# Norms and turns tile by tile, natural projections ahead of compress, dense tiles added during the last rows

## The chip, the cores and the metric

The kernel runs on one core of a Trainium2 chip. The time is device microseconds of one execution; the numbers compared are medians of several runs.

The engines are TensorE (PE, matmuls and transposes, here called turns; PEld is its weight load), VectorE (DVE), ScalarE (ACT), GpSimd (POOL) and SyncE (SP), which issues most DMAs. Each runs its own list of instructions in order and they meet by semaphores. Everything is fp32.

## The reference

A decoder layer for 512 tokens of width 1024: a combined projection, attention branches, and a retrieval of single-neuron experts (PEER), each after an RMSNorm, and a gated embedding at the end.

```python
h  = RMSNorm(x) ; z = h @ W_in
A  = sliding-window (128) GQA with per-head sinks and T5 relative bias
B  = compressed + selected blocks + sliding window (512), gated per head
x += W_o( sigmoid(gA) * (A @ W_upA) + sigmoid(gB) * (B @ W_upB) )
x += PEER(RMSNorm(x))
x += sigmoid(RMSNorm(x) @ W_pg) * (p @ W_ple)
out = RMSNorm(x)

def compress_blocks(t, pos, w1, w2):      # for B's compressed keys and values
    ...
    return jax.nn.gelu(flat @ w1) @ w2
```

## The kernel before

The 512 tokens are four tiles of 128 rows (TILES = 4), the width is KC = 8 chunks of 128. All orders are written out by hand: each engine has one function, and its instructions stand in program order.

**Start.** SP loads the x tiles, small constants, the bias table's two parts, then weight blocks of 512 KB. The blocks (wpack) go through a ring of RING = 5 places; block b is issued when block b - 5 has been used, which `used_up` expresses as a semaphore and a count. After block 0, SP waits for the bias rows, stores them and loads 16 bias tiles from them, before block 1. The PE makes the bias rows first (lines 1256 and 1257). ACT squares the four tiles (line 543) and takes one square root for all four (548). The DVE copies the bias rows out, fills `candno` (771), and scales the tiles (776). The PE turns them, chunk by chunk (1263), and ACT copies each chunk out to hT (552).

**Projections.** Thirteen blocks give z transposed (line 1272, ZT = 13, 8 matmuls each). For compress, the DVE builds windows of keys and values (788), and the PE multiplies them with eight blocks of w1 (1285), with 62 columns a matmul; four blocks are waited for at once and given back at once, one half (kv) after the other. ACT applies gelu (559). Then come the natural projections, values and head gates with tokens on the rows (1295): four blocks, all waited for first, 8 matmuls for each of the four tiles. The second compress matmuls (1301, 1304) follow, the DVE copies them out (793, 794), and the PE waits for that ahead of the first scores.

**Attention.** 32 batches: scores on the PE (1326), softmax on DVE, ACT and GpSimd, turned probabilities (1340) and values (1355). Between them the PE makes parts of the merge gates (1382). Then `up`, `project_out` (1415), which adds to x by `add_mixer` on the DVE (892), and `peer_norm`: ACT squares and roots, the DVE scales (899), the PE turns (1428), and queries (1453) follow.

**PEER.** Tiles 0 and 1 (NG = 2) gather rows of u and v, 512 KB for each of 128 picks a tile, by GpSimd's indirect DMAs (523) into SLOTS = 8 places; the DVE takes a product for each u row (1075) and adds each weighted v row (1110). A slot is gathered anew when its row has been used. Tiles 2 and 3 use all experts by dense matmuls: 128 chunks of scores (1542), then 128 chunks of values (1553), the matrix streamed by SP. At chunk 59 of the scores the PE turns the picks that the DVE numbered (1515). While rows of tile 1 are added (`accumulate(1, k)`, k = 0 to 127), dense tiles 2 and 3 are finished, and `add_dense` adds them to x.

**Tail.** In the order tile 0, 2, 3, 1 (`ORDER`; o counts them): ACT's square and root (`tail_norm`, 641, 643), the PE's turn (1480), the DVE's copy times gain (`tail_turned`, 1022), gate matmuls (1489), embedding matmuls (1503), ACT's sigmoid (650), the DVE's product and add (`tail_add`, 1030, 1033), ACT's last norm (656, 658), the last scaling (`tail_out`, 1039) and the store. `close(1)` ends tile 1's sum.

## Time and profile before

| | us |
|---|---|
| median of 3 runs | 1711.44 |
| the runs | 1711.39 to 1716.0 |
| the profiled execution | 1713.18 |
| its span in the trace | 1711.3 |
| PE busy | 1621.1 |
| DVE busy | 1064.0 |
| POOL busy | 619.8 |
| ACT busy | 431.0 |
| mean granted clock of the PE | 0.978 |

The span runs from the first to the last instruction; the execution's own time has a little around it. Busy times overlap between engines. The chain that ended last follows the work back from the last instruction, at each step to what released it. The granted clock is 1.00 at 2.4 GHz and 0.50 at 1.2 GHz. Up to 22 us the trace has no event of the clock, and the rows there say 1.00 whatever it was. A matmul in fp32 has two records.

### The profile page before, as it was taken

Reading aid. Unit: us, or ns where it says so; the run is one execution under the profiler, and the core shown is the slowest. Engines: PE = TensorE matmul, PEld = TensorE weight load, DVE = VectorE, ACT = ScalarE, POOL = GpSimd, SP = SyncE. Lnnn points to the kernel's source line nnn. Section 1 sums busy time; section 2 is a strip of 40 time slices with the busy share of each in tenths; the row PEclk is TensorE's granted clock in tenths of the full one; section 3 lists DMA queues with packets and bytes.
Section 4 is the critical chain, followed back from the end, with each engine's and each line's share of the span. In section 5 each row is a group of like instructions: output and inputs, shape, how many; then the busy total and the mean of one; then the engine's idle time right before and its main releaser. Section 6 shows DMA issues by size and latency. Waiting matters only on the chain.

```text
span 1711.3 us, 18283 instructions
## 1 busy us (share of the span) xinstructions
PE 1621.1 (95%) x6294; PEld 1052.1 (61%) x6294; DVE 1064.0 (62%) x2428; ACT 431.0 (25%) x1255; POOL 619.8 (36%) x650
## 2 busy tenths in 40 slices
PE   6988999998999799999989999999999999999957
PEld 3446454446588488888879999994444444444323
DVE  1010344442236999999968999997555556676772
ACT  3000444332011112111147777760000000000013
POOL 0000344460000144344445555555443344464620
PEclk9997999999999899999999999999999999999979
DMA  6231211004444699999989999999999999999940
GB/s 219 74 111 49 87 50 38 25 1 148 148 135 136 236 355 350 379 398 365 372 330 408 403 403 402 407 402 407 409 409 409 410 409 409 409 409 410 410 197 37
DMA packets 132552, 477.69 MB, mean 279 GB/s; under 512 B 14779, under 2 KB 15803, under 8 KB 132460
## 3 DMA queue, kind: packets, MB, share of 16 engines
q0 software_dynamic: 73728, 268.47, 40.0%
q1 hardware_dynamic: 58732, 208.06, 32.6%
q8 instruction: 50, 0.82, 0.2%
q14 instruction: 42, 0.34, 0.1%
HBM read 472.24 MB, written 4.24 MB: 278 GB/s over the span
## 4 chain that ended last, share of the span: by engine, by line
PE 65%; DMA 24%; DVE 4%; POOL 3%; issue 2%; ACT 1%; another core or an unknown queue 1%; SPq 0%; ACTq 0%; DVEq 0%
PE psum L1542 25%; DMA arena<-in_v,eidx 22%; PE psum L1453 6%; PE psum L1382 6%; PE psum L1272 5%; PE psum L1531 3%; PE psum L1415 3%; PE psum L1403 3%; PE psum L1489 2%; POOL arena L523 2%; PE psum L1340 2%; PE psum L1355 2%; PE psum L1295 1%; PE psum L1326 1%; PE psum L1285 1%
## 5 line engine op out<-in xcount | busy, mean ns | idle before, releaser
L1542 PE MATMUL psum<-arena 128*128 128x256 f32 x2048 | 455.2, 380 | 6.8 <-ACT arena L682 6.1
L1553 PE MATMUL psum<-arena 128*128 128x512 f32 x1024 | 440.8, 592 | 3.3 <-DMA arena<-in_vd 2.2
L523 POOL DMA_INDIRECT arena<-in_u,eidx x256 | 252.9, 988 | 474.7 <-DVE dots L1075 238.9
L1542 PEld LDWEIGHTS psum<-arena 128*128 128x128 f32 x2048 | 385.4, 191 | 57.4 <-issue 6.5
L523 POOL DMA_INDIRECT arena<-in_v,eidx x256 | 259.6, 1014 | 264.3 <-DVE arena L1110 147.8
L1553 PEld LDWEIGHTS psum<-arena 128*128 128x128 f32 x1024 | 194.2, 190 | 248.7 <-issue 242.5
L1110 DVE SCALAR_TENSOR_TENSOR arena<-arena,wts 128x1024 f32<-128x1024 f32 x182 | 233.2, 1285 | 118.9 <-DMA arena<-in_v,eidx 117.5
L1075 DVE CUSTOM_DVE_ANT_0 arena<-psum,arena 128x1024 f32<-128x1024 f32 x256 | 299.5, 1220 | 1.3 <-DVE arena L946 0.3
L501 POOL TENSOR_SCALAR arena<-arena 128x256 f32<-128x256 f32 (+4 forms) x128 | 105.9, 847 | 282.2 <-DVE arena L842 224.6
L1382 PE MATMUL psum<-arena 128*128 128x512 f32 x256 | 118.4, 605 | 0.0
L1453 PE MATMUL psum<-arena 128*128 128x256 f32 x512 | 113.0, 379 | 1.5 <-ACT arena L612 1.5
L1110 DVE SCALAR_TENSOR_TENSOR psum<-arena,wts,psum 128x1024 f32<-128x1024 f32 x57 | 73.5, 1289 | 52.7 <-DMA arena<-in_v,eidx 52.7
L1453 PEld LDWEIGHTS psum<-arena 128*128 128x128 f32 x512 | 96.2, 190 | 14.5 <-ACT arena L612 2.0
L705 ACT ACTIVATE arena<-arena 128x128 f32<-128x128 f32 x256 | 105.0, 488 | 0.0
L1272 PE MATMUL psum<-arena 128*128 128x512 f32 x208 | 89.5, 593 | 1.2 <-ACT arena L552 1.2
L682 ACT ACTIVATE arena<-psum 128x256 f32<-128x256 f32 (+31 forms) x126 | 41.1, 327 | 187.4 <-PE psum L1542 115.3
L641 ACT ACTIVATE arena<-arena 128x1024 f32<-128x1024 f32 x4 | 4.2, 1056 | 311.4 <-DVE arena L1117 252.3
L697 ACT ACTIVATE arena<-iota,arena 128x128 f32<-128x128 f32 x256 | 81.4, 395 | 0.0
L1382 PEld LDWEIGHTS psum<-arena 128*128 128x128 f32 x256 | 46.0, 189 | 55.5 <-issue 54.4
L588 ACT ACTIVATE arena<-arena 128x256 f32<-128x256 f32 (+4 forms) x128 | 59.8, 469 | 55.2 <-DVE arena L829 43.6
L1272 PEld LDWEIGHTS psum<-arena 128*128 128x128 f32 x208 | 39.4, 190 | 50.7 <-issue 49.3
L1531 PEld LDWEIGHTS psum<-arena 128*128 128x128 f32 x512 | 67.2, 192 | 3.3
(175 smaller groups left out, 1400.6 us busy)
## 6 DMA issues: line engine op xcount, KB each, us to landing
arena<-in_ut SPq DMA_DIRECT2D x128, 512.0 KB
arena<-in_vd SPq DMA_DIRECT2D x128, 512.0 KB
arena<-in_wpack SPq DMA_DIRECT2D x105, 512.0 KB
arena<-in_u,eidx POOLq DMA_INDIRECT x256
arena<-in_v,eidx POOLq DMA_INDIRECT x256
arena<-in_w_pg SPq DMA_DIRECT2D x8, 512.0 KB
arena<-in_x SPq DMA_DIRECT2D x4, 512.0 KB, 4.9
arena<-bias_rows SPq DMA_DIRECT2D x8, 256.0 KB, 5.6
```

Source lines behind the costliest of these rows:

```text
L501: last = G.tensor_scalar(sw[:, i % 3, r, 0:w], sw[:, i % 3, r, 0:w], scl[:, i, r:r + 1], None, ALU.mult)
L523: G.indirect_dma_start(out=row_slot(n), out_offset=None, in_=a["v"] if values else a["u"], in_offset=bass.IndirectOffsetOnAxis(ap=eidx[:, ...
L697: last = A.activation(hot2[:, g % 2, j, :], iota[:, :], ACT.Abs, scale=-1.0, bias=pickT[:, 1, tok:tok + 1])
L705: last = A.activation(hot2[:, g % 2, j, :], hot2[:, g % 2, j, :], ACT.Relu, scale=pickT[:, 3, tok:tok + 1], bias=pickT[:, 2, tok:tok + 1])
L1075: V.tensor_tensor_reduce(out=row_slot(n), in0=dot_rows[t], in1=row_slot(n), scale=1.0, scalar=0.0, op0=ALU.mult, op1=ALU.add, accum_out=do ...
L1110: V.scalar_tensor_tensor(to, row, w, to, ALU.mult, ALU.add).then_inc(row_used, 1)
L1272: last = T.matmul(ps[j % 8], blk(j)[:, k * P:(k + 1) * P], hT[:, k, :], start=(k == 0), stop=(k == KC - 1))
L1382: last = T.matmul(ps[4], blk(B_MG + m)[:, k * P:(k + 1) * P], hT[:, k, :], start=(k == 0), stop=(k == KC - 1))
L1453: last = T.matmul(ps[4 + p % 2][:, jj * HT:(jj + 1) * HT], blk(b)[:, k * P:(k + 1) * P], h2T[:, k, :], start=(k == 0), stop=(k == KC - 1))
L1531: last = T.matmul(mix_bank(g)[:, j * P:(j + 1) * P], hot1[:, g % 2, j, :], hot2[:, g % 2, j, :], start=True, stop=True)
L1542: last = T.matmul(chunk_scores(c), u[:, k * P:(k + 1) * P], h2T1[:, k, :], start=(k == 0), stop=(k == KC - 1))
L1553: last = T.matmul(ps[VALUE_BANK[t] + h], mixed[:, c, t * P:(t + 1) * P], stream[:, c % SRING, h * HALF:(h + 1) * HALF], start=(c == 0), st ...
```

## The change

The change moves work on four engines. (1) At the start ACT takes a root of a constant before x is there; ACT squares tiles 0 and 2, the DVE tiles 1 and 3; root, scaling and turning are made tile by tile. The bias matmuls move behind projection block 0, and SP's wait for the bias rows behind block 4. The bias table lies elsewhere, since its old place is written earlier now. (2) The natural projections come ahead of compress; they go by k in the outer loop, over four PSUM banks, and give back a block after each. Compress takes each block as it comes and gives it back when used, over two banks. The second compress matmuls stand behind the first two batches' scores and gate parts, and the DVE's copies of them behind batch 1's scores. (3) `peer_norm` has a root and a reciprocal for each tile, `turn` waits for one tile at a time, and for tiles 2 and 3 the scaling stands ahead of the second part of numbering the experts. (4) `add_dense` comes at rows 106 and 108 instead of 120 and 122, and the steps of the tail for tiles 2 and 3 follow among the rows. ACT's last norm of tile 2 moves ahead of the norm of tile 1.

```diff
-B_W1 = ZT
-B_NAT = B_W1 + 8
-B_MG = B_NAT + NATB
+B_NAT = ZT
+B_W1 = B_NAT + NATB
+B_MG = B_W1 + 8
...
             if b < ZT:
                 return proj_ready, b + 1
-            if b < B_NAT:
-                return cmp_hidden_ready, 2 * ((b - B_W1) // 4) + 2
+            if b < B_W1:
+                return (nat_block_used, b - B_NAT + 1) if b < B_W1 - 1 else (proj_ready, ZT + TILES)
             if b < B_MG:
-                return proj_ready, ZT + TILES
+                kv, part = divmod(b - B_W1, 4)
+                return (cmp_block_used, 3 * kv + part + 1) if part < 3 else (cmp_hidden_ready, kv + 1)
...
-                if b == 0:
+                if b == RING - 1:
...
-            for t in range(TILES):
+            def first_root(t):
+                A.activation(stat[:, 4 + t:5 + t], stat[:, t:t + 1], ACT.Sqrt, scale=1.0 / D,
+                             bias=epsc[:, :]).then_inc(rms_ready, 1)
+
+            A.activation(stat[:, 63:64], epsc[:, :], ACT.Sqrt)
+            for t in (0, 2):
                 act.wait_ge(x_loaded[t], 16)
                 norm_rows(t, 0, [early[:, i, :] for i in range(TILES)])
-            A.activation(stat[:, 4:8], stat[:, 0:4], ACT.Sqrt, scale=1.0 / D, bias=epsc[:, :]).then_inc(rms_ready, 1)
+                if t == 2:
+                    act.wait_ge(squares_ready, 1)
+                    first_root(1)
+                first_root(t)
+            act.wait_ge(squares_ready, 2)
+            first_root(3)
...
-            for j in range(4):
-                act.wait_ge(cmp_hidden_ready, j + 1)
-                A.activation(gT[:, j // 2, j % 2, :], ps[1 + j][:, 0:GROUPS * NCMP], ACT.Gelu_apprx_tanh).then_inc(cmp_gelu_ready, 1)
...
+            for kv in range(2):
+                act.wait_ge(cmp_hidden_ready, kv + 1)
+                for hb in range(2):
+                    last = A.activation(gT[:, kv, hb, :], hidden(kv, hb), ACT.Gelu_apprx_tanh)
+                last.then_inc(cmp_gelu_ready, 1)
...
-                A.activation(stat[:, 12 + t0:12 + t1], stat[:, 8 + t0:8 + t1], ACT.Sqrt, scale=1.0 / D,
-                             bias=epsc[:, :]).then_inc(rms_ready, 1)
+                    A.activation(stat[:, 12 + t:13 + t], stat[:, 8 + t:9 + t], ACT.Sqrt, scale=1.0 / D,
+                                 bias=epsc[:, :]).then_inc(rms_ready, 1)
...
             tail_gate(1)
+            tail_last_norm(1)
             tail_norm(3)
-            tail_last_norm(1)
             tail_gate(2)
...
+            def first_square(t):
+                dve.wait_ge(x_loaded[t], 16)
+                V.tensor_tensor_reduce(out=early[:, t, :], in0=xs[:, t, :], in1=xs[:, t, :], scale=1.0, scalar=0.0,
+                                       op0=ALU.mult, op1=ALU.add, accum_out=stat[:, t:t + 1]).then_inc(squares_ready, 1)
+
+            def first_norm(t):
+                dve.wait_ge(rms_ready, t + 1)
+                after(V.reciprocal(stat[:, 24 + t:25 + t], stat[:, 4 + t:5 + t]))
+                V.tensor_scalar(early[:, t, :], xs[:, t, :], stat[:, 24 + t:25 + t], None, ALU.mult).then_inc(rows_normed, 1)
+
+            first_square(1)
+            first_norm(0)
+            first_square(3)
+            for t in range(1, TILES):
+                first_norm(t)
...
+            def compressed_out():
+                dve.wait_ge(cmp_made, 1)
...
+                if i == 1:
+                    compressed_out()
...
-                dve.wait_ge(rms_ready, 2 + (t0 > 0))
-                after(V.reciprocal(stat[:, 28 + t0:28 + t1], stat[:, 12 + t0:12 + t1]))
                 for t in range(t0, t1):
+                    dve.wait_ge(rms_ready, TILES + t + 1)
+                    after(V.reciprocal(stat[:, 28 + t:29 + t], stat[:, 12 + t:13 + t]))
...
             add_mixer(3)
+            peer_norm(2, 4)
             number_low(0, 1)
-            number_high(0, 0)
-            peer_norm(2, 4)
-            for pair in range(1, 4):
+            for pair in range(4):
                 number_high(0, pair)
             publish(0, 4, 8, 0, 8)
...
-                if k == 120:
+                if k == 106:
                     add_dense(2)
-                if k == 122:
+                if k == 108:
                     add_dense(3)
                     tail_scale(1)
-                if k == 124:
+                if k == 110:
                     tail_turned(1)
-                if k == 126:
                     tail_scale(2)
+                if k == 112:
+                    tail_turned(2)
+                if k == 122:
+                    tail_add(1)
+                if k == 125:
+                    tail_out(1)
             close(1)
-            tail_turned(2)
-            tail_add(1)
             tail_scale(3)
-            tail_out(1)
             tail_turned(3)
             tail_add(2)
             tail_out(2)
...
-            pe.wait_ge(rel_loaded, 32)
             pe.wait_ge(pool_consts_set, 6)
-            pe.wait_ge(mask_row_set, 1)
-            T.matmul(ps[6][0:2 * HEADS, :], relb[:, :], hot[:, 0:HALF], start=True, stop=True)
-            T.matmul(ps[7][0:2 * HEADS, 0:P], relb[:, :], hot[:, HALF:S + P], start=True, stop=True).then_inc(bias_rows_ready, 1)
-            pe.wait_ge(bias_rows_out, 1)
-
-            pe.wait_ge(rows_normed, TILES)
-            for k in range(KC):
-                for t in range(TILES):
+            for t in range(TILES):
+                pe.wait_ge(rows_normed, t + 1)
+                for k in range(KC):
                     last = T.transpose(ps[k][:, t * P:(t + 1) * P], early[:, t, k * P:(k + 1) * P], ident[:, :])
-                last.then_inc(rows_turned, 1)
-
-            pe.wait_ge(hT_ready, KC)
+                    if t == TILES - 1:
+                        last.then_inc(rows_turned, 1)
+
             for j in range(ZT):
                 arrive(j)
+                if j == 6:
+                    pe.wait_ge(bias_rows_out, 1)
                 if j >= 8:
                     pe.wait_ge(proj_out, j - 7)
                 for k in range(KC):
+                    if j == 0:
+                        pe.wait_ge(hT_ready, k + 1)
                     last = T.matmul(ps[j % 8], blk(j)[:, k * P:(k + 1) * P], hT[:, k, :],
                                     start=(k == 0), stop=(k == KC - 1))
                 last.then_inc(proj_ready, 1)
+                if j == 0:
+                    pe.wait_ge(rel_loaded, 32)
+                    pe.wait_ge(mask_row_set, 1)
+                    T.matmul(ps[6][0:2 * HEADS, :], relb[:, :], hot[:, 0:HALF], start=True, stop=True)
+                    T.matmul(ps[7][0:2 * HEADS, 0:P], relb[:, :], hot[:, HALF:S + P], start=True,
+                             stop=True).then_inc(bias_rows_ready, 1)
+
+            pe.wait_ge(proj_out, ZT + TILES - 8)
+            for k in range(KC):
+                if k % 2 == 0:
+                    arrive(B_NAT + k // 2)
+                w = blk(B_NAT + k // 2)[:, (k % 2) * HALF:(k % 2) * HALF + NAT_COLS]
+                for t in range(TILES):
+                    last = T.matmul(ps[(ZT + t) % 8][:, 0:NAT_COLS], hT[:, k, t * P:(t + 1) * P], w,
+                                    start=(k == 0), stop=(k == KC - 1))
+                    if k == KC - 1:
+                        last.then_inc(proj_ready, 1)
+                if k % 2 and k < KC - 1:
+                    last.then_inc(nat_block_used, 1)
 
             for kv in range(2):
                 pe.wait_ge(windows_ready, 4 * kv + 4)
                 if kv == 0:
                     pe.wait_ge(proj_out, 11)
-                for b in range(4):
-                    arrive(B_W1 + 4 * kv + b)
+                else:
+                    pe.wait_ge(proj_out, 11 + TILES)
+                for l in range(LPAIR):
+                    b = B_W1 + 4 * kv + l // 4
+                    if l % 4 == 0:
+                        arrive(b)
+                    for hb in range(2):
+                        w = blk(b)[:, (l % 4) * CMP_HID + hb * P:(l % 4) * CMP_HID + (hb + 1) * P]
+                        last = T.matmul(hidden(kv, hb), w, cm[:, kv, l, :],
+                                        start=(l == 0), stop=(l == LPAIR - 1))
+                    if l == LPAIR - 1:
+                        last.then_inc(cmp_hidden_ready, 1)
+                    elif l % 4 == 3:
+                        last.then_inc(cmp_block_used, 1)
+
+            def compress():
+                pe.wait_ge(cmp_gelu_ready, 2)
                 for hb in range(2):
-                    for l in range(LPAIR):
...
-                    last.then_inc(cmp_hidden_ready, 1)
-
-            for b in range(NATB):
-                arrive(B_NAT + b)
-            for t in range(TILES):
-                j = ZT + t
-                for k in range(KC):
-                    w = blk(B_NAT + k // 2)[:, (k % 2) * HALF:(k % 2) * HALF + NAT_COLS]
-                    last = T.matmul(ps[j % 8][:, 0:NAT_COLS], hT[:, k, t * P:(t + 1) * P], w,
-                                    start=(k == 0), stop=(k == KC - 1))
-                last.then_inc(proj_ready, 1)
-
-            pe.wait_ge(cmp_gelu_ready, 4)
...
-            last.then_inc(cmp_made, 1)
...
+                last.then_inc(cmp_made, 1)
...
-            pe.wait_ge(cmp_out, 1)
-            pe.wait_ge(proj_out, 11 + TILES)
...
+            pe.wait_ge(cmp_gelu_ready, 1)
             for i in range(2):
                 queries_keys(i)
                 for part in range(4):
                     gate_part(i, part)
+            compress()
+            pe.wait_ge(cmp_out, 1)
             for i in range(len(BATCH)):
...
             def turn(h):
-                pe.wait_ge(rows_normed, TILES + 2 * h + 2)
-                for b in range(4):
-                    for kk in range(2):
-                        k = 2 * b + kk
-                        for t in range(2):
+                for t in range(2):
+                    pe.wait_ge(rows_normed, TILES + 2 * h + t + 1)
+                    for b in range(4):
+                        for kk in range(2):
+                            k = 2 * b + kk
                             last = T.transpose(ps[4 * h + b][:, (2 * kk + t) * P:(2 * kk + t + 1) * P],
                                                hn[2 * h + t][:, k * P:(k + 1) * P], ident[:, :])
-                    last.then_inc(rows_turned, 1)
+                        if t:
+                            last.then_inc(rows_turned, 1)
 
```

The PE from the start to the first turned probabilities, before (the L numbers are lines; the matmul with 16 rows is of the bias rows, 128x408 is natural, 128x62 compress, 64x62 and 31x64 its second part):

```order
L1256 MATMUL psum<-arena,relb 16x512
L1257 MATMUL psum<-arena,relb 16x128
L1263 MATMUL psum<-ident,arena 128x128 x32
L1272 MATMUL psum<-arena 128x512 x104
L1285 MATMUL psum<-arena 128x62 x64
L1295 MATMUL psum<-arena 128x408 x32
L1301 MATMUL psum<-arena,small 64x62 x2
L1304 MATMUL psum<-small,arena 31x64 x4
L1326 MATMUL psum<-arena 128x128 x4
L1382 MATMUL psum<-arena 128x512 x4
```

The same stretch now:

```order
L1293 MATMUL psum<-ident,arena 128x128 x32
L1306 MATMUL psum<-arena 128x512 x8
L1312 MATMUL psum<-arena,relb 16x512
L1313 MATMUL psum<-arena,relb 16x128
L1306 MATMUL psum<-arena 128x512 x96
L1322 MATMUL psum<-arena 128x408 x32
L1341 MATMUL psum<-arena 128x62 x64
L1376 MATMUL psum<-arena 128x128 x4
L1430 MATMUL psum<-arena 128x512 x4
L1376 MATMUL psum<-arena 128x128 x4
L1430 MATMUL psum<-arena 128x512 x4
L1351 MATMUL psum<-arena,small 64x62 x2
```

The bias matmuls went behind eight projection matmuls, the natural projections ahead of compress, and compress's second part behind two batches' scores and gates.

The DVE between the added output of tiles 2 and 3 (128x512 x4) and the end of numbering, before (the scaling of the norm is the SCALAR_TENSOR_TENSOR x2):

```order
L892 TENSOR_TENSOR arena<-arena,psum 128x512 x4
L975 TENSOR_TENSOR arena<-candno,arena 128x640
L977 TENSOR_TENSOR arena<-arena 128x640
L978 TENSOR_REDUCE arena<-arena 128x4x8
L975 TENSOR_TENSOR arena<-candno,arena 128x800
L977 TENSOR_TENSOR arena<-arena 128x800
L978 TENSOR_REDUCE arena<-arena 128x2x8
L897 RECIPROCAL stat<-stat 128x2
L899 SCALAR_TENSOR_TENSOR arena<-arena,stat 128x1024 x2
```

And now:

```order
L927 TENSOR_TENSOR arena<-arena,psum 128x512 x4
L933 RECIPROCAL stat<-stat 128x1
L934 SCALAR_TENSOR_TENSOR arena<-arena,stat 128x1024
L933 RECIPROCAL stat<-stat 128x1
L934 SCALAR_TENSOR_TENSOR arena<-arena,stat 128x1024
L1010 TENSOR_TENSOR arena<-candno,arena 128x640
```

Six instructions of the numbering moved from ahead of the two scalings to behind them.

The DVE's last rows, before (128x1024 with weights is a row; L1050 the dense add, L1022 the turned copy, L1117 the last sum, L1030 and L1033 gate product and add):

```order
L1110 SCALAR_TENSOR_TENSOR arena<-arena,wts 128x1024 x30
L1050 TENSOR_TENSOR arena<-arena,psum 128x512 x2
L1110 SCALAR_TENSOR_TENSOR arena<-arena,wts 128x1024 x2
L1050 TENSOR_TENSOR arena<-arena,psum 128x512 x2
L1017 RECIPROCAL stat<-stat 128x1
L1110 SCALAR_TENSOR_TENSOR arena<-arena,wts 128x1024 x2
L1022 TENSOR_TENSOR arena<-psum,small 128x512 x2
L1110 SCALAR_TENSOR_TENSOR arena<-arena,wts 128x1024 x2
L1017 RECIPROCAL stat<-stat 128x1
L1110 SCALAR_TENSOR_TENSOR arena<-arena,wts 128x1024
L1117 TENSOR_TENSOR arena<-arena 128x1024
L1022 TENSOR_TENSOR arena<-psum,small 128x512 x2
```

And now, from the second dense add on:

```order
L1085 TENSOR_TENSOR arena<-arena,psum 128x512 x2
L1052 RECIPROCAL stat<-stat 128x1
L1144 SCALAR_TENSOR_TENSOR arena<-arena,wts 128x1024 x2
L1057 TENSOR_TENSOR arena<-psum,small 128x512 x2
L1052 RECIPROCAL stat<-stat 128x1
L1144 SCALAR_TENSOR_TENSOR arena<-arena,wts 128x1024 x2
L1057 TENSOR_TENSOR arena<-psum,small 128x512 x2
L1144 SCALAR_TENSOR_TENSOR arena<-arena,wts 128x1024 x10
L1065 TENSOR_TENSOR arena<-arena,psum 128x512 x2
L1068 TENSOR_TENSOR arena<-arena 128x1024
L1144 SCALAR_TENSOR_TENSOR arena<-arena,wts 128x1024 x3
```

The dense adds stand 14 rows earlier, and a second turned copy, a gate product, an add and a last scaling have come in among the rows.

## Rows read from the trace of the kernel before

**Rows 1.** The page: shares of the chain; the costliest groups, the DVE's products.

```profile
PE 65%; DMA 24%; DVE 4%; POOL 3%; issue 2%; ACT 1%; another core or an unknown queue 1%; SPq 0%; ACTq 0%; DVEq 0%
...
L1075 DVE CUSTOM_DVE_ANT_0 arena<-psum,arena 128x1024 f32<-128x1024 f32 x256 | 299.5, 1220 | 1.3 <-DVE arena L946 0.3
```

**Rows 2.** The chain in order of time: start, duration, what.

```profile
15.09 2.75 DVE arena L776 x4
...
17.98 3.66 PE psum L1263 x16
...
24.79 89.53 PE psum L1272 x208
...
114.32 7.10 PE psum L1285 x64
...
127.68 13.90 PE psum L1285 x64
...
148.08 23.93 PE psum L1295 x64
...
548.78 27.48 PE psum L1415 x64
...
863.34 7.43 another core or an unknown queue
...
1652.36 27.47 PE psum L1489 x64
```

**Rows 3.** Timeline, 0 to 24 us: start, duration, engine, line, count [idle <-releaser].

```profile
4.51 1.28 ACT L543 ACT_TABLE_LOAD   x1 [4.51 <-DMA arena<-in_x]
...
10.51 1.28 ACT L548 ACT_TABLE_LOAD   x1
...
13.52 0.31 SPq L434 DMA_DIRECT2D bias_rows<-arena  x1
...
23.23 50.25 SPq L431 DMA_DIRECT2D arena<-in_wpack  x11
```

**Rows 4.** Line 423, x's DMAs: issue in ns, first and last start; landing.

```profile
L423 SPq DMA_DIRECT2D arena<-in_x x4: 392/422/432, 0.7 to 2.1; - x4
...
DMA to landing us min/median/max: 3.7/4.9/6.2
```

**Rows 5.** Stretches: window, busy of PE, PEld, DVE, ACT, POOL, clock, DMA, GB/s.

```profile
118.00:121.50 3.50, 3.41 (x31) 3.27 (x30) 0.00 (x0) 0.15 (x2) 0.00 (x0) 1.00 0.00 0
...
137.00:142.00 5.00, 4.56 (x22) 4.37 (x21) 0.00 (x0) 0.22 (x1) 0.00 (x0) 0.50 0.00 0
...
620.00:640.00 20.00, 20.00 (x103) 17.83 (x102) 19.59 (x27) 3.17 (x8) 7.73 (x9) 1.00 0.98 388
```

**Rows 6.** Timeline, the first scores on the PE.

```profile
173.76 0.72 PE L1326 MATMUL psum<-arena 64*128 64x128 f32 x8 [0.82 <-DVE arena L794]
```

**Rows 7.** Timeline, norms of tiles 2 and 3, and the picks' turn.

```profile
578.25 0.29 ACT L606 ACTIVATE stat<-stat,epsc 128x2 f32<-128x2 f32 x1
...
585.42 3.46 PE L1428 MATMUL psum<-ident,arena 128*128 128x128 f32 x16 [9.17 <-DVE arena L899]
...
589.56 10.63 PE L1453 MATMUL psum<-arena 128*128 128x256 f32 x48 [0.69 <-ACT arena L612]
...
857.53 0.41 PE L1515 MATMUL psum<-ident,arena 128*128 128x128 f32 x2 [0.48 <-issue]
```

**Rows 8.** Timeline, last 100 us: dense end, last rows, sum, add, last scaling.

```profile
1615.08 8.85 PE L1553 MATMUL psum<-arena 128*128 128x512 f32 x20 [1.52 <-DMA arena<-in_vd]
...
1617.80 23.04 DVE L1110 SCALAR_TENSOR_TENSOR arena<-arena,wts 128x1024 f32<-128x1024 f32 x18 [0.72 <-DMA arena<-in_v,eidx]
...
1640.75 1.28 DVE L1050 TENSOR_TENSOR arena<-arena,psum 128x512 f32<-128x512 f32 x2
...
1685.49 1.22 DVE L1033 TENSOR_TENSOR arena<-arena 128x1024 f32<-128x1024 f32 x1
...
1707.03 1.28 DVE L1039 SCALAR_TENSOR_TENSOR arena<-arena,stat 128x1024 f32<-128x1024 f32 x1
```

37 lines of the change are left out of this document (17 added, 20 removed).

## The prediction

> **What bounds the kernel now.** I read the chain of work that ended last first, because the shares of busy time are averages over stages that have different limits. It spends 65% of the span on TensorE (PE) and 24% on DMA [rows 1]. So a microsecond is worth something where that chain is on the PE, and nothing where another engine has spare time. Then I followed the chain in order of time through the three stretches that the diff touches.
>
> Stretch 1 is the start. The first projection matmul runs at 24.79 us [rows 2]. Before it stand the DVE's four scalings (15.09, 2.75 us, so 0.69 each), which wait for all four tiles' squares, and 32 turns on the PE from 17.98. Stretch 2 follows the projections: compress for keys at 114.32 (7.10 us), a wait for a block until 127.68, compress for values 13.90 us, another wait, and the natural projections from 148.08, 23.93 us. Stretch 3 is the end: the last DVE rows, then gate matmuls for tiles 2 and 3 (27.47 us) from 1652.36 and all that hangs on them [rows 2]. The norms of tiles 2 and 3, around 576 to 590 us, are a fourth place.
>
> **The start.** Before, ScalarE (ACT) loads a table at 4.51, squares four tiles, and loads a second one at 10.51 [rows 3]. The change asks for the square root's table before x lands and the listing has no second load. The x tiles land 3.7 to 6.2 us after issues at 0.7 to 2.1 us [rows 4]: the last at about 2.1 + 6.2 = 8.3. The DVE squares tile 3; the trace has no such square on the DVE, the nearest is a product with a sum over 1024 columns, 1.22 us [rows 1], so it is done at 9.6. Then come three scalings with a reciprocal each, about 0.9 apiece: 12.3. The PE turns tile 0 before that and starts on tile 1 at about 10.5. From there it is itself the late one: 24 turns at 3.66/16 = 0.229 us [rows 2] are 5.5 us, so the first projection starts at 16.0. The eight copies out of PSUM are fed to it one by one and hide under 0.86 us matmuls (89.53/104 [rows 2]). That is 8.8 us earlier. The two bias matmuls move from the idle start to behind block 0, where nothing hides them: 0.86 + 0.22 = 1.1 us. **Net gain 7.7.** SP is now held at block 4 for the bias rows instead of at block 0. Behind that wait are 16 bias tiles and block 5; before, SP went from storing the bias rows at 13.52 to the next block at 23.23 [rows 3], and block 5 is wanted 4 x 6.9 = 28 us after them, so those 10 us cost nothing. Bounds: 5 (the first block partly at 1.2 GHz, x tiles delayed by the four blocks behind them) and 9.5.
>
> **Natural projections ahead of compress.** From 114.32 to the end of the natural projections at 148.08 + 23.93 = 172.0 are 57.7 us. Now nothing in it should wait. Natural blocks are wanted one in 5.5 us and each is given back when used, and the first four compress blocks lie in the ring before compress starts. A compress block is used in 7.10/4 = 1.8 us; the fifth is wanted 7.1 us after its issue, and in the trace four blocks together landed between 121.4, when the ring was given back, and 127.68, in 6.3 us. The natural matmuls have 408 of 512 columns: 64 records x 0.430 x 408/512 = 21.9 us (the 23.93 holds a start at half clock). Compress is twice 7.10 = 14.2. The sum is 36.1. **Gain 21.6.** Of this 6.8 us hang on the clock. The granted clock was 1.00 until 121.5, while compress for keys ran, and 0.50 through compress for values [rows 5]: 1.2 instead of 2.4 GHz, after the PE had stood still. I take the high level for both halves, since the first half kept it for all its 7.1 us and fell only behind it; but the second half never brought it back in 13.9 us, so low work of this kind may also lose it in the end. That is a bound of +6.8, and of 13.6 if all of it ran low.
>
> One rule speaks against this order. Four accumulations in four banks now take turns within each k, and two within compress. In the trace the output projection does the same over four banks and its 64 records take 27.48 us [rows 2], 0.429 each, as those of the projections that stay in one bank (0.430). The Trainium skill, "TensorE: Matmul & The Clock Gate", section "A second HAM failure mode: psum-queue depth-cycling", says that going round PSUM banks leaves small gaps that make the clock swing between its levels. By that rule, the case of the low clock below would be the likely one; the row speaks against it.
>
> **The compressed keys** move behind the first two score and gate parts. The PE's 0.9 us of matmuls (173.76 - 0.82 - 172.0) and its wait of 0.82 us for the DVE's copies [rows 6] stay, only elsewhere. On the DVE the copies now stand ahead of the row scales of batch 1, which come some 2.7 us later; GpSimd and the PE's turn of batch 1 wait for those, but a gate part of 8 x 0.43 = 3.4 us stands between them on the PE. So zero, within 1 either way. Everything up to 575 us is then 7.7 + 21.6 = 29.3 us earlier, and the order of work there is unchanged.
>
> **Norms of tiles 2 and 3.** The root is there at 578.25, yet the PE starts turning at 585.42 after 9.17 us of idling, since the DVE numbers experts first [rows 7]. In the new order tile 2 is scaled by 578.4, tile 3 by 580.0, and queries start near 583 instead of 589.56: 6.5 us on the PE. I give it **zero**, as the DVE is late next. From 600 to 860 it is busy 19.3 to 19.8 us in every 20 (one row stands for thirteen [rows 5]), and its work is what the PE waits for at the turning of the picks: idle 0.48 us at 857.53 [rows 7]. The PE will come 6.5 us early and stand there. The DVE has 0.3 us more (a reciprocal, a wait for tile 3's root): **cost 0.3.**
>
> The same edit for tiles 0 and 1 is covered: the PE works on the second half's `up` while they are normed.
>
> **The end.** Dense work ends at 1615.08 + 8.85 = 1623.93, and the last 18 rows take 1.28 us each [rows 8]. Row 106 is 14 rows before 1640.75, so at 1622.9. There the first dense tile is added (1.28), two more rows follow, and the second tile is added at 1626.8, after the dense end, so no wait. The PE turns tile 2 at 1624.2 and tile 3 from 1628.1 to 1629.1, makes the embedding (4 matmuls of 0.86, 3.4), and starts the gates at 1632.6; the DVE's turned copy is ready at 1632.1. Against 1652.36 [rows 2] that is 19.8. The PE stands for about 3 us between the two turns and may lose its clock, 0 to 3 us; I take 1: **gain 18.8.** What is late next: the last tile's sum. The DVE gets 1.28 + 1.28 + 1.22 + 1.45 = 5.2 us more before it (turned copy and gate product, priced like the dense add of two halves out of PSUM; the add over 1024 columns; the last scaling with its reciprocal [rows 8]), so it closes near 1659.5. The PE wants it when gates 1 and 2 are done, at 1632.6 + 1 + 27.5 = 1661.1. That holds by 1.6 us.
>
> **Sum.** 7.7 + 21.6 - 0.3 + 18.8 = 47.8 us. The profiled execution took 1713.18 (span 1711.3), which is 1.7 above the median of the runs; 1665.4 for it, and 1711.44 - 47.8 = 1663.6 for the median. The DMA-bound stage between 1165 and 1640 starts earlier by the same amount and has the same bytes to move, so it passes the shift on.
>
> **Rivals.**
> *Low clock in compress.* For: the second half ran 13.9 us without getting the clock back. Against: the first half kept it. It costs 6.8 to 13.6: 1671 with the second half alone.
> *The gap at the picks closes.* Behind the picks ACT stands idle for reasons the profile doesn't name, 7.43 us from 863.34 [rows 2], and the PE waits for it. If ACT, coming 6.5 us early, has this behind it while the PE waits for the DVE, then 6 to 8 us of the norm's gain come through: about 1657.
> *The end gives only part.* The dense end comes later relative to the rows, or the PE restarts at 1.2 GHz (10 us passed from the first dense sum at 1642.0 to the gates at 1652.36 [rows 2, 8]), and the DVE stands at row 122 for the gates with everything behind it. Half of the gain less: about 1672.
> *The shift is swallowed.* If the rows between 1165 and 1640, 24% of the chain on DMA [rows 1], have a pace of their own that the earlier start doesn't move, only the end's gain stays: about 1693.
> *Slower.* The add at row 108 waits for the last dense values. The DVE, the eight gather slots and GpSimd's next gathers stand with it, microsecond for microsecond, once these values come over 3 us later than in the trace; the whole gain is gone from 51 us on, some 15 dense chunks. While the gathers stand, the stream has the DMA for itself, which speaks against it. At 55 us late it gives 1716.
>
> **How the numbers follow.** Forecast 1664, its own range 1659 to 1669: 0.59. Gap at the picks closes: 0.15. End only in part: 0.12. Low clock: 0.10. Shift swallowed: 0.03. Slower: 0.01. The range of 8 in 10 reaches from 1654 to 1678; it holds the first four with their bounds. A measurement of this kernel can tell a change of about 0.3%, 5 us. All but the slower case lie beyond it; with something left for what I have not seen: faster 0.97, within 0.3% 0.01, slower 0.02.
>
> **What would show it.** Right: first projection at 16 us; the clock at 1.00 from there to the first scores, at about 144; PE idle some 7 us before the turning of the picks, with the DVE as releaser; the gates for tiles 2 and 3 some 10 us behind the dense end instead of 28.4 (1652.36 - 1623.93), and the last sum closed before the PE asks. Wrong: a clock of 0.50 in the natural or compress stage, PE waits for blocks there, DVE waits on the PE at rows 106 to 122, or a distance from the first score to the first dense value that has changed by more than 3 us.

## The result and the profile after

The changed kernel takes 1663.86 us (median, 1658.48 to 1664.06) beside 1713.72 us for the kernel before: a ratio of 0.9704, 95% interval 0.9689 to 0.9719. A second comparison on another occasion gave 1660.88 beside 1711.82 us, 0.9700 (0.9687 to 0.9713). The prediction was 1664, from a saving of 47.8 us; measured were 49.9 and 50.9 us. The profiled execution took 1663.66 us, its span 1661.9, at a mean granted clock of 0.993 (0.978 before).

The page's shares of the chain have hardly moved from [rows 1]:

```profile
PE 67%; DMA 23%; DVE 4%; POOL 2%; issue 2%; ACT 1%; SPq 0%; ACTq 0%; DVEq 0%
```

The chain in order of time (start, duration, what) answers to [rows 2]:

```profile
10.33 3.62 PE psum L1293 x17
...
14.86 7.11 PE psum L1306 x16
...
23.15 82.60 PE psum L1306 x192
...
105.75 21.92 PE psum L1322 x64
...
127.67 14.24 PE psum L1341 x128
```

The last three stand back to back: 12 projection blocks, the natural projections, both halves of compress. In the kernel before, this stretch held two waits for blocks. The stretches of the changed kernel (window, busy time of PE, PEld, DVE, ACT, POOL, granted clock, DMA share, GB/s) answer to [rows 5]:

```profile
105.70:127.70 22.00, 22.00 (x68) 12.24 (x66) 2.69 (x4) 1.53 (x3) 0.00 (x0) 1.00 0.31 95
127.70:134.80 7.10, 7.10 (x66) 7.10 (x65) 0.00 (x0) 3.64 (x8) 0.00 (x0) 1.00 0.73 216
134.80:142.00 7.20, 7.20 (x66) 7.13 (x67) 0.00 (x0) 0.39 (x3) 0.00 (x0) 1.00 0.87 296
```

The timeline of the PE (start, duration, engine, line, count, idle before and its releaser) at `up` and at the norms of tiles 2 and 3, the turning of the picks and the first mix, where [rows 7] stood before:

```profile
372.03 8.14 PE L1454 MATMUL psum<-arena 128*128 128x256 f32 x29 [2.33 <-DMA arena<-in_wpack]
...
550.46 1.07 PE L1479 MATMUL psum<-ident,arena 128*128 128x128 f32 x8 [2.27 <-DVE arena L934]
...
554.59 1.78 PE L1505 MATMUL psum<-arena 128*128 128x256 f32 x7 [1.50 <-ACT arena L633]
...
829.84 0.66 PE L1567 MATMUL psum<-ident,arena 128*128 128x128 f32 x2 [6.40 <-issue]
...
847.18 1.05 PE L1583 MATMUL psum<-arena 128*128 128x128 f32 x8
```

And the end, on the PE, where [rows 8] stood:

```profile
1581.66 8.85 PE L1605 MATMUL psum<-arena 128*128 128x512 f32 x20 [1.44 <-DMA arena<-in_vd]
1592.48 1.09 PE L1532 MATMUL psum<-ident,arena 128*128 128x128 f32 x8 [1.98 <-DVE arena L1085]
1596.07 1.97 PE L1532 MATMUL psum<-ident,arena 128*128 128x128 f32 x8 [2.49 <-DVE arena L1085]
1597.83 5.03 PE L1555 MATMUL psum<-arena 128*128 128x512 f32 x8
1602.70 27.63 PE L1541 MATMUL psum<-arena 128*128 128x512 f32 x64
1630.17 1.04 PE L1532 MATMUL psum<-ident,arena 128*128 128x128 f32 x8
```

How much earlier each place comes than in the trace of before, in us:

| place | before | after | earlier |
|---|---|---|---|
| second projection block (24.79 + 89.53/13) | 31.7 | 23.15 | 8.5 |
| end of natural projections and compress | 172.0 | 141.9 | 30.1 |
| last half tile of `add_mixer` | 576.3 | 548.2 | 28.1 |
| queries of tiles 2 and 3 | 589.56 | 554.59 | 35.0 |
| first turn of picks | 857.53 | 829.84 | 27.7 |
| first mix | 880.28 | 847.18 | 33.1 |
| end of the dense values | 1623.93 | 1590.51 | 33.4 |
| gates of tiles 2 and 3, by the chain | 1652.36 | 1602.86 | 49.5 |
| end of the span | 1711.3 | 1661.9 | 49.4 |

The table tells where to ask: the first two rows are the start and the middle; the shift then falls by 2.0, rises and falls by 7 around the norms of tiles 2 and 3, gains 5.4 between the picks and the first mix, which no term of the sum had, and 16.1 at the end.

### The profile page after: what moved, and what is told of

The parts are those of the page before. It is cut to its first block, busy times and chain, and to the rows that moved or that the text cites. A ratio compares the mean times of both kernels' runs of the same rounds, so it can differ in the third digit from the quotient of the medians.

```text
span 1661.9 us, 18284 instructions
## 1 busy us (share of the span) xinstructions
PE 1611.3 (97%) x6294; PEld 1043.6 (63%) x6294; DVE 1066.2 (64%) x2437; ACT 428.0 (26%) x1256; POOL 622.6 (37%) x650
## 4 chain that ended last, share of the span: by engine, by line
PE 67%; DMA 23%; DVE 4%; POOL 2%; issue 2%; ACT 1%; SPq 0%; ACTq 0%; DVEq 0%
PE psum L1594 27%; DMA arena<-in_v,eidx 23%; PE psum L1505 7%; PE psum L1430 6%; PE psum L1306 5%; PE psum L1583 3%; PE psum L1466 3%; PE psum L1454 3%; PE psum L1541 2%; PE psum L1390 2%; PE psum L1405 2%; POOL arena L532 1%; PE psum L1376 1%; DVE arena L1144 1%; PE psum L1322 1%
## 5 line engine op out<-in xcount | busy, mean ns | idle before, releaser
L1306 PEld LDWEIGHTS psum<-arena 128*128 128x128 f32 x208 | 39.4, 190 | 49.4 <-issue 48.7
```

The lines of the kernel that those rows point to most:

```text
L1306: last = T.matmul(ps[j % 8], blk(j)[:, k * P:(k + 1) * P], hT[:, k, :], start=(k == 0), stop=(k == KC - 1))
```

## Experiments

Each kernel below was timed beside the kernel before on the same chip. In the comparison of the second four (bulk_return, only_norms, turn_at_61, embeds_ahead) that kernel ran at 1705.44 us, 7 us below the other comparisons, and no trace of it was taken there. For these four I compare with each other, and by place in the trace, not by ratio.

A ratio carries about 0.0015 either way. The difference of two of them therefore carries about 3.6 us, and a range such as "8.4 to 9.1" below only says which of the two ratios of the changed kernel (0.9704 or 0.9700) was taken.

### The start, the middle and the end, each undone alone

old_start puts the old start back:

```diff
-            A.activation(stat[:, 63:64], epsc[:, :], ACT.Sqrt)
-            for t in (0, 2):
+            for t in range(TILES):
                 act.wait_ge(x_loaded[t], 16)
                 norm_rows(t, 0, [early[:, i, :] for i in range(TILES)])
...
+            A.activation(stat[:, 4:8], stat[:, 0:4], ACT.Sqrt, scale=1.0 / D, bias=epsc[:, :]).then_inc(rms_ready, 1)
...
-            first_square(1)
-            first_norm(0)
...
+            pe.wait_ge(bias_rows_out, 1)
+            pe.wait_ge(rows_normed, TILES)
```

> The changed kernel with the start as before (one root for all four tiles, turns chunk by chunk, bias matmuls ahead, the wait for the bias rows behind block 0). The trace of the changed kernel has the second projection block at 23.15 us against 31.7. Theory (the start passes on whole): 8.6 us slower than the changed kernel, 1672.5. Rival (a stall behind the picks depends on when the streams meet, and opens again when everything comes later): 5 us more, 1677.5. Rival (the start is swallowed later): 1664.

1670.5 us beside 1712.73, ratio 0.9753 (0.9738 to 0.9768). Against the two ratios of the changed kernel that is 0.0049 to 0.0053 of 1712.7, **8.4 to 9.1 us**. The traces are finer: the second projection block comes at 32.1 us (23.2 to 23.5 in the changed kernel and in embeds_ahead), the last half tile of `add_mixer` at 555.9, which is 8.6 us behind embeds_ahead and 7.7 behind the trace of the changed kernel, where `up` ran into the low clock (see below). So the start passes on whole, and the rival that had it swallowed (1664) falls. From the first turn of picks to the first mix are 17.3 us, as in the changed kernel (17.3), so the stall behind the picks does not return with a later start, and the first rival falls too.

old_middle puts compress ahead again, with its blocks waited for and given back four at a time, and makes the compressed keys before the first scores:

```diff
-B_NAT = ZT
-B_W1 = B_NAT + NATB
+B_W1 = ZT
+B_NAT = B_W1 + 8
...
-                if i == 1:
-                    compressed_out()
```

> The changed kernel with compress ahead of the natural projections again, its blocks waited for and given back four at a time, and the compressed keys made before the first scores. Theory (57.7 us instead of 36.2 for the stretch, with the second half of compress at a granted clock of 0.50): 21.5 us slower than the changed kernel, 1685.4. Rival (the low clock came from where the stretch lay in time, not from the PE's wait for blocks; with the earlier start it stays at 1.00): 14.7 us slower, 1678.6.

1682.72 us, ratio 0.9827 (0.9812 to 0.9842): **21.1 to 21.8 us**. Its PE timeline has both waits and the slow half, 9 us earlier in time than in the kernel before [rows 2]:

```profile
104.86 7.25 PE L1319 MATMUL psum<-arena 128*128 128x62 f32 x64
118.33 13.89 PE L1319 MATMUL psum<-arena 128*128 128x62 f32 x64 [6.21 <-DMA arena<-in_wpack]
138.37 23.81 PE L1329 MATMUL psum<-arena 128*128 128x408 f32 x64 [6.16 <-DMA arena<-in_wpack]
```

So the low clock came back with the waits, though the stretch ran 9 us earlier, and the rival (14.7 us) falls.

old_end puts the dense sums back to rows 120 and 122, with the steps of the tail behind them:

```diff
-                if k == 106:
+                if k == 120:
                     add_dense(2)
-                if k == 108:
+                if k == 122:
                     add_dense(3)
                     tail_scale(1)
```

> The changed kernel with the dense tiles added at rows 120 and 122 again and the tail's steps where they were. Theory (16.4 us of the shift arise between the end of the dense values and the end of the span): 16.4 us slower than the changed kernel, 1680.3. Rival (the sum of the prediction, 18.8 us, the rest being lost to other places): 1682.7. Rival (the last rows of tile 1 bound the end in both orders): under 10 us slower, below 1674.

1681.16 us, ratio 0.9809 (0.9794 to 0.9824): **18.0 to 18.7 us**, nearer to the prediction's 18.8 than to the 16.4 that I had expected from one pair of traces, though the interval holds both. In its PE timeline the PE stands 19.93 us and then stays slow until the gates:

```profile
1609.43 1.97 PE L1530 MATMUL psum<-ident,arena 128*128 128x128 f32 x8 [19.93 <-DVE arena L1085]
1613.02 1.97 PE L1530 MATMUL psum<-ident,arena 128*128 128x128 f32 x8 [1.62 <-DVE arena L1085]
1614.78 5.59 PE L1553 MATMUL psum<-arena 128*128 128x512 f32 x8
1620.21 25.05 PE L1539 MATMUL psum<-arena 128*128 128x512 f32 x58
```

From the dense end (1580.65 + 8.85) to the end of the span are 89.9 us here, 87.4 in the kernel before, 71.4 in the changed kernel and 69.5 in its second trace. The 2.5 us between the first two are mostly a longer wait for the dense sum (19.93 us instead of 18.15), and 0.7 us of low clock in the embedding (5.59 instead of 4.92). The last two differ by a wait (1.98 and 1.06 us) and by the clock: the embedding behind the turns took 5.03 us in the one and 4.09 us in the other. By traces the end is thus worth anything from 16.0 to 20.4 us, and the last rival (under 10 us) falls. The three parts undone add up to 47.5 to 49.6 us of the 49.9 and 50.9, which fits, given the intervals, but is no proof that nothing else takes part.

### What brings the low clock in compress

bulk_return keeps the new order, but compress waits for four blocks at once and gives back four at once:

```diff
-                kv, part = divmod(b - B_W1, 4)
-                return (cmp_block_used, 3 * kv + part + 1) if part < 3 else (cmp_hidden_ready, kv + 1)
+                return cmp_hidden_ready, (b - B_W1) // 4 + 1
...
+                for i in range(4):
+                    arrive(B_W1 + 4 * kv + i)
                 for l in range(LPAIR):
                     b = B_W1 + 4 * kv + l // 4
-                    if l % 4 == 0:
-                        arrive(b)
```

> The changed kernel, order and all, but each half of compress waits for its four blocks at once and gives them back at once. Theory (in the second half it is the PE's wait for blocks that brings the low clock): the PE waits some 6 us ahead of the second half, and the half then runs at 0.50 and takes 13.9 us instead of 7.1; together 12 to 13 us slower than the changed kernel, 1676. Rival (the clock is lost only when the wait comes before the natural projections, or the earlier start keeps it): the wait alone, 5 to 6 us, 1669.5.

1673.29 us. turn_at_61 and embeds_ahead, timed beside it, are the changed kernel up to the picks: their last half tile of `add_mixer` comes at 547.4 us in both, that of bulk_return at 561.7. So the edit costs **14.3 us**. The PE's timeline, and one stretch of it:

```profile
126.84 7.25 PE L1340 MATMUL psum<-arena 128*128 128x62 f32 x64
140.34 13.88 PE L1340 MATMUL psum<-arena 128*128 128x62 f32 x64 [6.24 <-DMA arena<-in_wpack]
154.15 1.23 PE L1373 MATMUL psum<-arena 64*128 64x128 f32 x8
155.31 5.43 PE L1427 MATMUL psum<-arena 128*128 128x512 f32 x8
```

```profile
127.00:134.00 7.00, 7.00 (x65) 6.96 (x63) 0.00 (x0) 3.64 (x7) 0.00 (x0) 1.00 0.26 77
134.00:140.00 6.00, 0.10 (x1) 0.00 (x0) 0.00 (x0) 0.34 (x2) 0.00 (x0) 0.58 0.81 294
140.00:155.00 15.00, 14.66 (x72) 14.57 (x72) 0.00 (x0) 0.72 (x3) 0.00 (x0) 0.50 0.05 22
```

The wait is 6.24 us, the half behind it takes 13.88 us at 0.50 where the changed kernel needs some 7.1 at 1.00, and the first scores and gate matmuls are slow too (1.23 and 5.43 us; 0.71 and 3.70 in the changed kernel), which I had not counted. That makes 6.2 + 6.8 + 2.2 = 15.2, less 1.0 us by which this trace's stretch began earlier than in the two beside it: 14.2. The same matmuls on the same data keep the high level when nothing stops the PE ahead of them, so the rival (5 to 6 us) falls. So more than half of the middle's 21.5 us hangs on taking and giving back blocks one by one: the new order alone leaves one of the two waits and the slow half. The other half of the question, the old order with blocks given back one by one, was not run.

### The norms of tiles 2 and 3, and the gap behind the picks

old_norms scales tiles 2 and 3 behind the second part of numbering again; old_norms_again is the same kernel, timed beside after_again, the changed kernel itself. only_norms makes the opposite edit in the kernel before:

```diff
-            peer_norm(2, 4)
             number_low(0, 1)
-            for pair in range(4):
+            number_high(0, 0)
+            peer_norm(2, 4)
+            for pair in range(1, 4):
```

> The changed kernel with the scaling of tiles 2 and 3 behind the second part of numbering again; the roots stay tile by tile. Theory A (the DVE bounds the way to the picks, and the PE's gain of 6.5 us is returned there; the smaller gap behind the picks has another cause): no difference within 1 us, 1663.9. Theory B (the gap behind the picks shrank because ACT and the PE come early and have it behind them while they wait for the DVE): 5 to 6 us slower, 1669, and the trace shows the ACT idle behind the picks and the PE waiting some 6 us for it.

> The changed kernel with tiles 2 and 3 scaled behind the second part of numbering, a second time, beside the changed kernel itself. Where the standstill behind the picks is absent: the PE comes 6.9 us later but the picks are turned at the same time, so no difference within 1 us, or 1 to 2 us faster, as the scaling before numbering cost the kernel before 2.4 us. Where it is present: up to 4 us slower than the changed kernel.

> The kernel before with one edit: tiles 2 and 3 are scaled ahead of the second part of numbering (one root for both, as before). Theory A (the DVE bounds the way to the picks and the gap behind them is no part of this edit): no difference within 1 us of before. Theory B (the edit lets the PE and ACT wait ahead of the turning of the picks, and the gap behind it shrinks from 22.8 to about 17.3 us, from the first turn of picks to the first mix): 4 to 5.5 us faster than before, a ratio of 0.997 to 0.9975.

> The changed kernel, unchanged, beside the others of this comparison. If the 5.4 us that came through behind the picks are a matter of the chip, then beside a kernel before of 1705 it stands 44 to 45 us lower, near 1661, a ratio of 0.9740; beside one of 1712 near 1664, 0.9705. Rival (they belong to the order of the norms): 0.9705 in both cases, 1655 beside 1705.

> The kernel before, unchanged, for its trace beside the others of this comparison. Question: its runs stood at 1711 to 1717 us in two comparisons and at 1704 to 1707 in a third, while one edit of the norms made it 2.4 us slower there. Theory (the standstill of ACT and the PE behind the picks comes and goes with the chip, not with the kernel's order): where this kernel runs near 1705, its trace has no such standstill, and first turn of picks to first mix is near 16 us; where it runs near 1712, it is near 22.8. Rival (the standstill belongs to the kernel's order, and the 7 us between chips come from another stage, such as the DMA-bound one from 1165 on): 22.8 us in either case.

old_norms took 1664.55 us, ratio 0.9712 (0.9699 to 0.9725), the second time 1662.46, 0.9716 (0.9701 to 0.973), against 1660.88 for after_again. By the ratios that is 1.4 and 2.7 us dearer than the changed kernel, by the medians of the second comparison 1.6; the intervals overlap, so neither is clear of zero. only_norms took 1708.03 us beside 1705.44: 2.6 us slower, ratio 1.0014 (1.0005 to 1.0023), where theory A had none and theory B a gain. 1.1 to 1.6 us of that lie ahead of the edit (its last half tile of `add_mixer` comes at 577.3, before at 576.3 and 575.7); the rest fits a kernel before that had no standstill to lose in that comparison, but no trace shows it. before_again took 1710.42 beside 1711.82, 0.9994 (0.9985 to 1.0004), the scatter of the method; its 20.3 us behind the picks are neither the 16 of its theory nor the 22.8 of its rival.

First the DVE. From the last half tile of `add_mixer` to the first turn of picks are 281.3 and 280.9 us in the two traces of before, 281.6 and 281.3 in those of after, 281.3 and 281.2 with the old place of the scaling. The PE comes 5 to 6 us earlier in the new order and the picks are turned at the same time. In after_again and old_norms_again, one row each:

```profile
830.19 0.66 PE L1567 MATMUL psum<-ident,arena 128*128 128x128 f32 x2 [7.41 <-DVE arena L1041]
```

```profile
829.67 0.41 PE L1568 MATMUL psum<-ident,arena 128*128 128x128 f32 x2 [1.18 <-issue]
```

Theory A's half on the DVE is shown: the gain on the PE is handed back, and the price is at most 0.4 us, no more than two traces of one kernel differ by.

Then the gap. At the high clock and without any standstill the first mix would come some 14.5 us behind the first turn (0.7 us of turns, four chunks of 3.46). What is more than that is the PE standing, or its low clock. The traces have:

| kernel | place of the scaling | first turn to first mix | of it the PE stands | this run, us |
|---|---|---|---|---|
| before | late | 22.8 | 6.1 | 1713.18 |
| before_again | late | 20.3 | 3.8 | 1710.42 |
| old_norms | late | 21.5 | 4.6 | 1666.94 |
| old_norms_again | late | 16.4 | 1.6 | 1661.41 |
| after | early | 17.3 | 1.2 | 1663.66 |
| after_again | early | 17.1 | 0.8 | 1661.83 |
| only_norms | early | 16.2 | none | 1708.42 |
| old_start, old_middle, old_end | early | 17.3, 17.3, 17.2 | none, 1.1, none | 1670.47, 1682.08, 1681.20 |
| bulk_return, embeds_ahead | early | 15.8, 17.4 | none, none | 1673.07, 1656.47 |

ACT's timeline in old_norms, the long case (start, duration, engine, line, idle before and its releaser):

```profile
830.09 0.38 ACT L703 ACTIVATE arena<-psum 128x256 f32<-128x256 f32 x1 [4.70 <-remote]
833.00 0.60 ACT L735 ACTIVATE arena<-psum 128x512 f32<-128x512 f32 x1 [2.52 <-remote]
...
841.66 0.38 ACT L703 ACTIVATE arena<-psum 128x256 f32<-128x256 f32 x1 [7.52 <-remote]
843.16 0.38 ACT L703 ACTIVATE arena<-psum 128x256 f32<-128x256 f32 x1 [1.12 <-remote]
```

The second row copies the picks out, which the PE had turned by 830.7. The third reads the scores of chunk 59, ready at about 834.0 (the PE's two chunks after the turns took 7.07 us from 830.50). At these places the program has ACT wait for the PE alone, yet the trace names no engine. With the early scaling seven of eight traces lie between 16.2 and 17.4, and one at 15.8; with the late one four lie anywhere from 16.4 to 22.8, two of them from the same program (21.5 and 16.4). So it is no property of the order alone: the standstill comes in different lengths from run to run, and where ACT and the PE wait 5 to 7 us for the picks anyway, most of it is over by then.

The wait for the picks has a price of its own. With the early scaling the PE stands 4.7 to 7.4 us ahead of the picks, and the granted clock is low behind that. In old_start, where the PE does not stand again before the first mix:

```profile
838.00:842.00 4.00, 4.00 (x14) 3.37 (x13) 4.00 (x7) 1.15 (x3) 2.43 (x3) 0.50 1.03 422
...
843.00:855.00 12.00, 11.87 (x56) 10.15 (x55) 4.91 (x10) 4.45 (x14) 4.70 (x5) 1.00 1.03 410
```

Its 17.3 us are the 14.5 plus 2.8 us of low clock; in the eight early traces this part is 1.3 to 2.9 us (the third column less the fourth and 14.5), in the four late ones, behind the standstill, 0.3 to 2.4. So the early scaling shortens the standstill from between 1.6 and 6.1 us to at most 1.2, but keeps the low clock. That fits theory B's mechanism, with too few traces of the late order to show it; its price fails: not 5 to 6 us but 1.4 to 2.7. What ACT waits for stays open; no kernel here tells it.

### Using the PE's wait ahead of the picks

```diff
-TURN_AT = 59
+TURN_AT = 61
```

> The changed kernel with one number changed: the picks are turned at chunk 61 of the dense scores instead of 59. The PE spends the 6.40 us for which it stood ahead of the picks on chunks 59 and 60, which then no longer lie behind them. Theory (the idle time is real slack of the PE, and dense scores pass a shift on): up to 6.4 us faster than the changed kernel, 1657.5 to 1660. Rival (ACT's unnamed standstill takes place whenever it has not stood waiting for the picks, and takes back what is gained): no difference, or slower, 1663 to 1669, with ACT idle 5 to 8 us behind the picks.

1654.33 us (1652.59 to 1655.0), the fastest of its comparison. In its PE timeline the wait is gone and the first mix comes 7.6 us behind the first turn, two chunks and no standstill:

```profile
829.87 0.38 PE L1567 MATMUL psum<-ident,arena 128*128 128x128 f32 x2
...
837.44 1.05 PE L1583 MATMUL psum<-arena 128*128 128x128 f32 x8
```

The changed kernel itself was not run beside it, and by ratio (0.9696 against 0.9700 and 0.9704) the edit gains nothing; but the kernel before was 7 us low in this comparison, so its worth can only be read by place. embeds_ahead ran beside it and is the changed kernel up to the dense end: the dense values start at 1120.4 us here and at 1128.2 there, 7.8 us earlier, yet the dense end is only 3.5 us earlier (1585.4 and 1588.9). The loss has a place. Tile 0's gates, among the dense values, here and then in embeds_ahead:

```profile
1468.21 15.67 PE L1541 MATMUL psum<-arena 128*128 128x512 f32 x32 [2.56 <-DVE arena L1057]
```

```profile
1473.42 13.90 PE L1541 MATMUL psum<-arena 128*128 128x512 f32 x32
```

The PE waits 2.56 us for the DVE's turned copy, and the gates behind it take 1.8 us more at the low clock (0.59 from 1468 to 1472): 4.3 us together, the whole loss. The gathered rows did start 7.8 us earlier too (the DVE's first row into SBUF at 1123.08 and 1130.93), but the copy that stands among them came at 1466.79 and 1469.54, only 2.8 us earlier; between them the DVE waits again and again for gathers, at a DMA share of 1.03 (1464 to 1472). In the other 13 traces the dense values take 459.8 to 460.7 us from start to end, here 465.1. The rival's standstill did not come in this trace; it did in both_edits.

### Filling the PE's waits at the end

embeds_ahead computes tile 3's embedding ahead of the turn of tile 2, and tile 1's ahead of the last turn. both_edits keeps the first, has tile 1's behind the last turn again, and adds the edit of turn_at_61. This is the order of both_edits against the changed kernel (the DVE's wait for the embeddings goes with it):

```diff
+            tail_embed(2)
             tail_turn(1)
             tail_turn(2)
             tail_embed(1)
             tail_gate(1)
             tail_gate(2)
             tail_turn(3)
-            tail_embed(2)
             tail_embed(3)
```

> The changed kernel with the embedding of tile 3 computed ahead of the turn of tile 2, and that of tile 1 ahead of turning tile 1. The tile 3 embedding fills the PE's two waits of 1.98 and 2.49 us for the dense sums, behind which the granted clock was 0.50. Theory (the PE bounds the end; 3.4 us of embedding leave the path, and the clock stays high, some 1.5 us): 4 to 5 us faster than the changed kernel, 1659 to 1660. Rival (the last row of tile 1 closes at 1627.9, and the PE, now earlier, waits there): at most 3 us faster, 1661, with the DVE as releaser of the last turn.

> The changed kernel with the picks turned at chunk 61 and the embeddings of tiles 3 and 1 moved (that of tile 3 ahead of the turn of tile 2, that of tile 1 behind the turn of tile 1's last sum, where it covers the DVE's copy). Theory: 6.5 us from the picks (turn_at_61 against the changed kernel), and the PE's waits of 0.23 and 2.49 us at the end filled by 3.4 us of embedding, 2.6 us: 9 us faster than the changed kernel, a ratio of 0.9645 to 0.9690. Rival (the DMA-bound stage or the last row of tile 1 takes the second gain back, with the DVE as releaser of the last turn): as turn_at_61 alone, 6.5 us.

embeds_ahead took 1655.87 us. From the dense end to the end of the span are 65.7 us, against 71.4 and 69.5 in the traces of the changed kernel: **3.8 to 5.7 us**, as the first theory said. (By ratio, 0.9707, nothing shows, as with turn_at_61.) both_edits took 1655.36 us beside 1711.82, ratio 0.9668 (0.9653 to 0.9684), **5.5 us faster than the changed kernel** in the same comparison and not 9. Its PE timeline at the end has no half clock and one wait of 0.66 us, 65.1 us from the dense end to the end of the span:

```profile
1579.65 8.85 PE L1605 MATMUL psum<-arena 128*128 128x512 f32 x20 [1.39 <-DMA arena<-in_vd]
1588.34 3.60 PE L1555 MATMUL psum<-arena 128*128 128x512 f32 x8
1591.78 1.04 PE L1532 MATMUL psum<-ident,arena 128*128 128x128 f32 x8
1593.47 1.09 PE L1532 MATMUL psum<-ident,arena 128*128 128x128 f32 x8 [0.66 <-DVE arena L1085]
```

The lost part is at the picks: the dense values start at 1128.2, as in embeds_ahead, so TURN_AT = 61 gained nothing in this trace. ACT copies the picks out at 838.59, 8 us after they were turned, and the first mix comes 13.1 us behind the first turn instead of 7.6:

```profile
838.59 0.60 ACT L735 ACTIVATE arena<-psum 128x512 f32<-128x512 f32 x1 [3.87 <-remote]
```

The code up to there is that of turn_at_61. With the wait for the picks gone, nothing covers the standstill when it comes. One trace without it and one with it do not tell how often that is.

## Why the prediction was right, and where it was not

**The start** was put at 7.7 us; the traces have 8.5, the runs 8.4 to 9.1. The first projection starts at 14.86 where I had 16.0: the 24 turns took 4.37 us, 0.18 each, and not 0.229, the price of 16 turns in [rows 2], which were fed by the DVE. The bias matmuls and a block of 7.11 us instead of 6.89 took some of that back. SP's wait at block 4 cost nothing. One reading was wrong: the DVE's four scalings did not wait for the four squares. In the kernel before, the root was there by 12.1 us, and the DVE was still copying bias rows and filling `candno`:

```profile
11.80 0.30 ACT L548 ACTIVATE stat<-stat,epsc 128x4 f32<-128x4 f32 x1
...
13.42 1.55 DVE L771 COPY candno<-iota 128x8 f32<-128x8 f32 x24
```

The reciprocal came at 14.9. By these rows 2.8 of the us won at the start, an estimate, come from having this work behind the scalings, not from going tile by tile. The sum built up the new time from other rows, so it was not touched.

**The middle** was put at 21.6 us; the traces have 21.5 (57.7 less 36.2), the runs 21.1 to 21.8. The terms fit one by one: natural 21.92 (21.9), compress 14.24 (14.2), the clock at 1.00 in both halves. That the low clock in compress comes with the PE's wait was argued in the prediction and is shown by bulk_return. The natural projections went round four banks for 22 us at a clock of 1.00, and so did compress over two for 14.2 us; nothing of a clock that swings is seen. The Trainium skill ("TensorE: Matmul & The Clock Gate", section "A second HAM failure mode: psum-queue depth-cycling") tells of a bf16 kernel with 512 columns that lost the high level by going round PSUM banks. Read as a rule for this kernel, as the prediction weighed it, that would have cost the high level here; the trace disagrees.

**The compressed keys** were put at zero within 1: the turn of batch 1 comes 30.0 us earlier (182.22 before, 152.22 after) against 30.1 at the end of compress, so they cost 0.1.

**What the sum did not have.** The matmuls of `up` lose 1.6 us. The PE waits for blocks there in both kernels, 2.73 us before and 2.33 after, but only after does the clock fall; this is the stretch in the changed kernel:

```profile
372.00:374.00 2.00, 1.97 (x5) 1.61 (x6) 0.00 (x0) 0.00 (x0) 0.00 (x0) 0.50 1.02 418
```

The prediction called the order of work up to 575 us unchanged and let the shift pass; the clock is not passed on that way. It is not a fixed cost of the change either. Eight traces have this code up to here. In four the clock is low behind the wait (these matmuls take 26.0 to 26.1 us). In the other four it is low in the 16 matmuls ahead of it, which shortens the wait, and the rest takes 24.4 us as in the kernel before; embeds_ahead is one of them:

```profile
366.36 5.29 PE L1454 MATMUL psum<-arena 128*128 128x256 f32 x16 [0.79 <-DVE arena L896]
372.78 24.44 PE L1454 MATMUL psum<-arena 128*128 128x256 f32 x112 [1.13 <-DMA arena<-in_wpack]
```

**The norms of tiles 2 and 3.** The gain on the PE was put at 6.5 (6.9 measured), the cost at 0.3 (at most 0.4), and the PE was to stand some 7 us for the DVE ahead of the picks: 6.40, where the trace names no releaser, and 7.41 in after_again, where it names the DVE. Right, step by step, but for the low clock that such a wait brings, which the sum did not price. The case "gap at the picks closes" was set beside it at 0.15, as if either it or the forecast had to come true. Part of it came true along with the forecast: 5.4 us in the one pair of traces, 1.4 to 2.7 by the runs.

**The end** was put at 18.8 us: 16.1 to the gates in the first pair of traces, 18.0 to 18.7 by the runs. The low clock, taken at 1 us, cost 2.3 in the first trace: a turn of 1.97 instead of 1.09 and an embedding of 5.03 instead of 3.60. The dense end came 33.4 us earlier, but the add behind row 106 only 31.7 (1591.15, where the prediction had 1622.9 in the old time), so the PE stood 1.98 us for it. The gates start 12.2 us behind the dense end; I had 9.7 with that 1 us. The last sum did close in time, at 1626.71 + 1.22 = 1627.9, ahead of the PE's 1630.17, a margin of 2.2 us where I had 1.6.

So 47.8 against the 49.4 us of the two spans hides errors of both signs: +0.8 at the start, -2.0 up to 548 us, +5.4 behind the picks, -2.7 at the end. The near hit is partly luck, and the time itself doubly so: 1663.6 was counted from a median of 1711.44 for the kernel before, which stood at 1713.72 with a fourth run, while the saving was 2 us larger than forecast. "The shift is swallowed" is refuted for this change (33.1 us at the start of the dense values, 33.4 at their end); turn_at_61 shows how a shift can be lost there all the same, where the PE meets a step of the DVE that stands among gathered rows.

## What to carry to other kernels

When a stage waits for a bulk of blocks, price the wait and the stretch behind it: here a wait of 6.2 us cost 9 us more through the clock, and giving blocks back one by one removed both. A gain on an engine that is not late next comes back as idle time there, and the low clock behind that idle time costs extra (1.3 to 2.9 us here). Look whether other work can be put into it, and whether it has been covering another engine's standstill. Split the measured total at six or eight places before calling a prediction right, since a sum can agree while its terms do not.
